# Attention inside a two-layer decoder block: heads scored in blocks of four over four PSUM banks, and the q units confined to one pair of banks

## The reference, cut to what matters

```python
proj = h @ w_in + b_in                       # layer 0
s = q k^T - slope * dist                     # two blocks of 128 queries
m = max(max(s), sink); e = exp(s - m)
p = e / (sum(e) + exp(sink - m))
o = p v;  mix = o @ w_o + b_o
...
proj = h @ w_in                              # layer 1
p_cmp = masked_softmax(q k_cmp^T - slope * d_cmp)
p_sel = masked_softmax(...);  p_win = masked_softmax(...)
o = g0 * p_cmp v_cmp + g1 * p_sel v_sel + g2 * p_win v_win
mix = o @ w_o
...
x = x + rmsnorm(mix);  x = x + rmsnorm(conv_ffn(rmsnorm(x)))
```

## Time and profile before

| | |
|---|---|
| median of 3 runs | 2155.23 us (2155.08 to 2158.4) |
| the profiled execution | 2156.59 us, span of the core 2154.9 us |
| mean granted clock of PE | 0.998 |
| PE busy | 2142.0 us, 99% of the span |
| DVE, ACT, POOL busy | 1330.8, 1067.6, 206.8 us |
| the chain that ended last | PE 97%, DVE 2%, ACT 1% |
| attention stretches (first host slot to the last output) | 57.8 to about 200 us in layer 0, 1138.1 to about 1336 us in layer 1 |

### The profile page before, as it was taken

How to read it: one execution, slowest core, us unless ns; L and a number is a source line. 1 busy time by engine, 2 the same in 40 slices (tenths; PEclk the granted TensorE clock), 3 DMA queues, 4 the chain that set the end, 5 groups by cost and what they waited for, 6 DMA issues and landing times.

```text
span 2154.9 us, 34701 instructions
## 1 busy us (share of the span) xinstructions
PE 2142.0 (99%) x12323; PEld 1833.1 (85%) x12323; DVE 1330.8 (62%) x2019; ACT 1067.6 (50%) x1611; POOL 206.8 (10%) x355
## 2 busy tenths in 40 slices
PE   9999999999999999999999999999999999999999
PEld 9987788888888888888898887788888888888887
DVE  7655676676766754446855554576676666754443
ACT  6675464444444444434556666464444444444343
POOL 3231000000000000002103442000000000000000
PEclk9999999999999999999999999999999999999999
DMA  7444446555565565554673233545556556565553
GB/s 249 140 164 142 164 166 205 185 184 193 168 204 185 185 214 187 189 191 157 215 237 102 86 109 115 178 166 180 200 175 195 185 181 198 177 214 189 191 185 127
DMA packets 107216, 381.42 MB, mean 177 GB/s; under 512 B 14114, under 2 KB 14578, under 8 KB 106482
## 3 DMA queue, kind: packets, MB, share of 16 engines
q1 hardware_dynamic: 104962, 373.69, 51.6%
q10 hardware_dynamic: 2160, 6.46, 0.8%
HBM read 377.97 MB, written 2.14 MB: 176 GB/s over the span
## 4 chain that ended last, share of the span: by engine, by line
PE 97%; DVE 2%; ACT 1%; DMA 0%; issue 0%; SPq 0%; ACTq 0%; DVEq 0%
PE set L599 32%; PE set L663 31%; PE set L603 16%; PE set L775 10%; PE set L843 1%; PE set L824 1%; PE set L867 1%; PE set L706 1%; PE set L826 0%; PE set L870 0%; PE set L860 0%; DVE block_f L1810 0%; DVE wlo L1467 0%; PE set L904 0%; PE set L905 0%; PE set L815 0%
## 5 line engine op out<-in xcount | busy, mean ns | idle before, releaser
L1467 DVE TENSOR_TENSOR wlo<-raw,whi 128x1024 fp32r<-128x1024 f32 x704 | 856.7, 1227 | 585.0 <-ACT whi L1075 583.4
L1075 ACT ACTIVATE whi<-raw 128x1024 fp32r<-128x1024 f32 x704 | 738.4, 1057 | 729.3 <-PE set L603 351.3
L599 PE MATMUL set<-hs,whi 128*128 128x512 f32 x2944 | 976.2, 396 | 2.0 <-DVE hs L1523 2.0
L603 PE MATMUL set<-hs,wlo 128*128 128x256 f32 x2944 | 697.7, 280 | 0.0
L603 PEld LDWEIGHTS set<-hs,wlo 128*128 128x128 f32 x2944 | 547.2, 188 | 63.1
L599 PEld LDWEIGHTS set<-hs,whi 128*128 128x128 f32 x2944 | 504.5, 188 | 71.5 <-DVE hs L1523 3.2
L663 PE MATMUL set<-whi,hid 128*128 128x512 f32 x1408 | 387.2, 395 | 0.0
L663 PEld LDWEIGHTS set<-whi,hid 128*128 128x128 f32 x1408 | 264.9, 188 | 63.2 <-DVE wlo L1467 0.6
L663 PE MATMUL set<-wlo,hid 128*128 128x512 f32 x704 | 222.6, 395 | 0.0
L775 PE MATMUL set<-hs,whi 128*128 128x256 f32 x1280 | 214.6, 289 | 0.0
L775 PEld LDWEIGHTS set<-hs,whi 128*128 128x128 f32 x1280 | 176.7, 189 | 8.3 <-issue 5.5
(11 more groups left out here) (178 smaller groups left out, 1301.9 us busy)
## 6 DMA issues: line engine op xcount, KB each, us to landing
raw<-in_stream SPq DMA_DIRECT2D x704, 512.0 KB, 3.3
gain_rows<-rows ACTq DMA_DIRECT2D x4, 1024.0 KB, 4.8
xT<-in_x SPq DMA_DIRECT2D x8, 256.0 KB, 7.3
out_y<-out_f SPq DMA_DIRECT2D x3, 512.0 KB, 2.6
bo_rows<-rows ACTq DMA_DIRECT2D x1, 1024.0 KB, 8.1
wg_raw<-in_w_gates ACTq DMA_DIRECT2D x1, 768.0 KB, 5.2
out_y<-out_f SPq DMA_DIRECT2D x2, 256.0 KB, 3.2
w2k_sb<-in_w ACTq DMA_DIRECT2D x2, 128.0 KB, 7.4
```

Source lines behind the costliest of these rows:

```text
L599: return mm(sets[set_of(u)][:, t, 0:2 * w], whi[:, slot, cols], r, start=first, stop=final)
L603: return mm(sets[set_of(u)][:, t, w:2 * w], wlo[:, slot, cols], r[:, 0:w], start=False, stop=False)
L1075: A(whi[:, slot, :], raw[:, slot, :], ACT.Copy).then_inc(hi_ready, 1)
L1467: V.tensor_tensor(wlo[:, slot, :], raw[:, slot, :], whi[:, slot, :].bitcast(F32), ALU.subtract).then_inc(lo_ready, 1)
```

## The change

Two pairs of heads make a block (8 blocks in layer 0, 16 in layer 1). PE makes the scores of the block's four heads in one run in four banks, banks 0 and 1 of `set1` and banks 2 and 3 of `set0`, and right behind them the outputs of the block two before. The four turns of the block before stand one by one in later slots. `block_slots` writes down by hand in which slot each block starts (`at`), at which offsets ACT and DVE take its heads (`scored`), and at which offsets the turns stand (`turned`). The compressed scores of layer 1 get a slot of their own, three slots ahead of the block (two in the last group). `turned` moves into the space of `half`, `probs` is twice as large.

Since `set0` banks 2 and 3 now hold scores, all q units accumulate in banks 0 and 1. PE's first products of a q unit wait for the first half of the q read of the unit before, its seventh product waits for the second half (slots 0 and 1). The first output unit waits for the whole of the last q read, in layer 0 with its bias. The second output unit waits for DVE to have read the last scores.

```diff
+def block_slots(layer):
+
+    if layer == 0:
+        at = [CH * UT * g + o for g in range(GROUPS - 1) for o in (4, 18)]
+        scored, turned = [(0, 3, 6, 9)] * len(at), [(1, 4, 7, 10)] * len(at)
+        last = (3, 12)
+        scored, turned = scored + [(0, 2, 4, 6)] * 4, turned + [(1, 3, 5, 7)] * 4
+    else:
+        at = [CH * UT * g + o for g in range(GROUPS - 1) for o in (6, 13, 20, 26)]
+        scored, turned = [(0, 2, 3, 5)] * len(at), [(1, 3, 4, 5)] * len(at)
+        last = (4, 9, 14, 19)
+        scored, turned = scored + [(0, 1, 3, 4)] * 4 + [(0, 2, 3, 5)] * 2, turned + [(1, 2, 3, 4)] * 4 + [(1, 3, 5, 7)] * 2
+    at += [CH * UT * (GROUPS - 1) + o for o in last + (26, 36)]
+    return at, scored, turned
...
+    for b in range(BLOCKS[layer] + 2):
+        first_of_group = layer == 1 and b % 4 == 0 and b < BLOCKS[layer]
+        if first_of_group:
+            put(scoring, at[b] - (3 if b // 4 < GROUPS - 1 else 2), (b, COMPRESSED))
+        if layer == 1 and b % 4 == 1 and b < BLOCKS[layer]:
+            put(turning, at[b], (b - 1, COMPRESSED))
+        for k in range(4):
+            put(scoring, at[b] + scored[b][k], (b, k))
+            if 1 <= b <= BLOCKS[layer]:
+                put(turning, at[b] + turned[b][k], (b - 1, k))
+    return scoring, turning
...
-        ps_scores = [sets[1][:, 0, :], sets[1][:, 1, :]]
+        ps_scores = [[sets[1][:, 0, :], sets[1][:, 1, :]], [sets[0][:, 2, :], sets[0][:, 3, :]]]
...
-                            pe.wait_ge(evacuated, UT * (u - 1))
+                            pe.wait_ge(evacuated, UT * (u if u in (O0, O1) else u - 1))
...
+                    if (k, c) == (1, 0):
+                        pe.wait_ge(scores_read, items_through(0 if u == O0 else 1, PAIRS[0 if u == O0 else 1] - 1))
...
-                    if kt == KT - 1:
+                    if kt == KT - 1 or kt == 0 and u not in (KS1, KW1):
...
-                            if u in (Q0 + 1, KW1):
-                                pe.wait_ge(rnorm_ready, 1 if u < KW1 else 3)
-                            if u in (Q1, Q1 + 1):
-                                pe.wait_ge(evacuated, UT * ((KS1 if u == Q1 else KW1) + 1))
-                            elif u in (Q0 + 2, Q0 + 3, Q1 + 2, Q1 + 3):
-                                pe.wait_ge(evacuated, UT * (u - 1))
+                            if u == KW1:
+                                pe.wait_ge(rnorm_ready, 3)
+                            if u == Q1:
+                                pe.wait_ge(evacuated, UT * (KS1 + 1))
+                        if kt == 0 and n in (0, 6):
+
+                            if Q0 < u < O0:
+                                pe.wait_ge(q_scaled, UT * (u - Q0 - 1) + (2 if n == 0 else 4))
+                            if Q1 < u < O1:
+                                pe.wait_ge(evacuated, UT * (u - 1) + (2 if n == 0 else 4))
...
-                second = u == KW1 or (u - (Q0 if u < O0 else Q1)) % 2 == 1 and u != KS1
-                return [2, 3] if second else [0, 1]
+                return [2, 3] if u == KW1 else [0, 1]
...
-                    for m, h in at[tile]:
-                        if LAG <= m < PAIRS[layer] + LAG and h < len(pair_heads(layer, m - LAG)):
-                            turn(m - LAG, h)
-                        if h == 0 and m < PAIRS[layer]:
-                            scores(m)
-                        if h == 0 and LAG + 1 <= m:
-                            outputs(m - LAG - 1)
+                    for b, k in scoring[tile]:
+                        if k == COMPRESSED:
+                            scores(compressed_pair(b), 0)
+                        if k == 0 and b < BLOCKS[layer]:
+                            for n, m in enumerate(block_pairs(layer, b)):
+                                scores(m, n)
+                        if k == 0 and b >= 2:
+                            if layer == 1 and (b - 2) % 4 == 0:
+                                outputs(compressed_pair(b - 2), 0)
+                            for n, m in enumerate(block_pairs(layer, b - 2)):
+                                outputs(m, n)
+                    for b, k in turning[tile]:
+                        if k == COMPRESSED:
+                            turn(compressed_pair(b), 0)
+                        else:
+                            turn(block_pairs(layer, b)[k // 2], k % 2)
...
-                        o = m - LAG - 1
-                        if h == 1 and o >= 0 and pair_item(layer, o)[1] in ("swa", "win"):
-                            pair_high(o)
-                        if LAG <= m < PAIRS[layer] + LAG and h < len(pair_heads(layer, m - LAG)):
-                            copy_turned(m - LAG, h)
-                        if m < PAIRS[layer] and h < len(pair_heads(layer, m)):
-                            exponents(m, h)
+                    for b, k in turning[tile]:
+                        if k == COMPRESSED:
+                            copy_turned(compressed_pair(b), 0)
+                        else:
+                            copy_turned(block_pairs(layer, b)[k // 2], k % 2)
+                    for b, k in scoring[tile]:
+                        if k == COMPRESSED:
+                            continue
+                        if k == 0 and b < BLOCKS[layer] and layer == 1 and b % 4 == 0:
+                            exponents(compressed_pair(b), 0)
+                        if b < BLOCKS[layer]:
+                            exponents(block_pairs(layer, b)[k // 2], k % 2)
+                        if k == 1 and b >= 2:
+                            pairs = block_pairs(layer, b - 2)
+                            act.wait_ge(o_ready, items_through(layer, pairs[1]))
+                            for n, m in enumerate(pairs):
+                                if pair_item(layer, m)[1] != "sel":
+                                    pair_high(m, n)
...
-                        if h == 0:
-                            if 1 <= m < PAIRS[layer] + 1:
-                                reciprocals(m - 1)
-                            if m < PAIRS[layer]:
-                                for k in range(len(pair_heads(layer, m))):
-                                    add_bias(m, k)
+                    for b, k in scoring[tile]:
+                        if k == COMPRESSED:
+                            add_bias(compressed_pair(b), 0)
                             continue
-                        o = m - LAG - 1
-                        if o >= 0 and pair_item(layer, o)[1] in ("swa", "win"):
-                            pair_low(o)
+                        if k == 0 and 1 <= b <= BLOCKS[layer]:
+                            reciprocals(block_pairs(layer, b - 1)[1])
+                        if k == 1 and layer == 1 and b % 4 == 0 and b < BLOCKS[layer]:
+                            reciprocals(compressed_pair(b))
+                        if b < BLOCKS[layer]:
+                            if k == 2:
+                                reciprocals(block_pairs(layer, b)[0])
+                            add_bias(block_pairs(layer, b)[k // 2], k % 2)
+                        if k == 2 and b >= 2:
+                            for n, m in enumerate(block_pairs(layer, b - 2)):
+                                if pair_item(layer, m)[1] != "sel":
+                                    pair_low(m, n)
...
+                        if g > 0:
+                            dve.wait_ge(scores_ready, items_before(layer, g))
+                        bank = sets[0][:, half_unit, :]
```

More of the change, by code:

```diff
@@ new lines, in attention_steps, with put @@
+def attention_steps(layer):
+    slots = CH * UT
+    at, scored, turned = block_slots(layer)
+    hosts = [[[] for _ in range(slots)] for _ in range(GROUPS - 1)] + [[[] for _ in range(LAST_SLOT + 1)]]
+    scoring = hosts
+    turning = [[[] for _ in h] for h in hosts]
+    def put(where, slot, what):
+        host = min(slot // slots, GROUPS - 1)
+        where[host][slot - host * slots].append(what)
+    for b in range(BLOCKS[layer] + 2):
[9 more added lines that the diff above has]
+    return scoring, turning
@@ L1218, in attention @@
             def attention(layer, host):
-                at = attention_steps(layer)[host]
+                scoring, turning = [steps[host] for steps in attention_steps(layer)]
                 def copy_turned(m, h):
```

117 lines of the change are left out of this document (60 added, 57 removed).

## The result

The changed kernel takes **2181.5 us** (median of 4 runs, 2176.7 to 2182.1) against 2156.7 for the kernel before (4 runs): a ratio of 1.0112, 95% interval 1.0101 to 1.0124. It is slower by 1.1%, 1.5 us under the forecast of 2183. The profiled execution has a span of 2180.4 us, 25.5 more than before.

The account below looks back on a forecast made before the run. PE's own queue was taken as the bound. Saving -5, removed wait -0.7, layer 0 waits +12.6, layer 1 +18.9, correction -0.8 made +25; clock +3 gave +28 on 2156.6, 2184.6, less 1.4 for the median: 2183 us, range 2169 to 2193.

Parts of the forecast that it names:

- The waits at the q units: Layer 0, third and fourth q unit and first output unit: PE waits 2.7, 2.7 and 4.4 us for q read or bias.
- The waits for copies: Layer 1: turns wait for ACT's copies behind exponents and splits; with q read and score waits, 18.9 us in all.
- with 0.8 taken off: Correction of 0.8 us, because walking the kernel before gave waits of 1.1 and 0.5 where its trace has 0.7 and nothing.
- the signs: What would show it: waits about 30 us, about 1 us at layer 1's unit starts, a block's run about 3.5 us.
- The saving on PE: Both layers: fewer entries and exits of attention runs save 5 us in all, ends 2 and 9.
- one run of 2 x 1.65: PE's run per block: scores and outputs of two pairs priced at 1.65 us per pair, before entry and exit.
- The clock: Behind three waits of 2.7 us or more the granted clock falls, 1.7 us lost each: 3 us, ends 0 and 5.1.
- the removed one: Layer 0, first output unit: the 0.7 us wait of the fifth chunk for a stored output goes.
- The rule against the trace: Scores in different row halves and banks could run in parallel by the skill's rule: 20 us back, 2163; 3 in 100.
- The waits were not hidden: Rival that waits are hidden and only the saving stays, making the kernel faster: 2150 us; chance 6 in 100.
- no third of them vanished: Rival that the walk overstates, a third to half of the waits vanishing: +9 to +16, 2164 to 2171; chance 13.
- that rival: Clock falls after waits of 1 to 2 us too: eight more, 1.7 us each, up to 2197; chance 8.

Follow-up runs that it names:

- e1: Changed kernel with DVE's q read moved ahead of the low split of the chunk before last, in all host units of both layers: 2170.9 us.
- e7: Changed kernel with one number changed, the second block of a host unit of layer 0 at slot 16 instead of 18: 2173.5 us.
- e4: Changed kernel with only layer 0's table of slots changed (second block at 17, output unit blocks at 0, 12, 23, 34): 2165.6 us.
- e3: Changed kernel with only layer 1's table of slots changed (a pair's two heads taken together, last blocks respaced): 2168.6 us.
- again: Changed kernel once more, unchanged, for another profiled execution: 2180.5 us.
- e6: Changed kernel with layer 0's new table, layer 1's shifted again, q read and gate inversion moved, first output unit of layer 0 not waiting for q bias: 2153.2 us.
- e8: Kernel with both tables and everything moved, but each run takes scores, outputs, scores, outputs pair by pair: 2159.7 us.
- e12: Kernel before, with the score products of both heads of a pair on the first head's rows: 2186.3 us.
- e2: Kernel before with only the q units' banks changed to a single set, with the changed kernel's waits for read and q bias: 2163.8 us.
- e5: Changed kernel with both new tables of slots, layer 0's and layer 1's: 2156.4 us.
- e9: Kernel with both tables and everything moved, with score products of both heads of a pair on the first head's rows: 2182.0 us.

## Why the prediction was right, and where it was not

**The waits at the q units** were walked at 2.7, 2.7 and 4.4. They are marked 2.56, 2.53 and 4.39; read as above, they are 2.72, 2.69 and 4.55. Chain, place and size were right, shown by moving the read (e1), the block (e7) and the table (e4). All waits of layer 0 were put at 12.6 and are 11.8.

**The waits for copies** were right in place and cause, shown by e3. Layer 1 was walked at 18.9, with 0.8 taken off, and lost 16.7 in marked waits. By host unit: 5.9 forecast, 5.1 marked in five waits, so 5.9; then 4.2 forecast each, 2.83 and 2.87 marked in four waits each, so 3.5; then 4.5 against 2.98 marked in five, 3.8. The walked waits for the reads of the third and fourth unit are not marked, but PE's timeline has them:

```profile
1199.91 0.28 PE L830 MATMUL set<-hs,wlo 128*128 128x256 f32 x1
1200.33 0.50 PE L830 MATMUL set<-hs,whi 128*128 128x256 f32 x2
```

The start comes 0.41 after the product before it instead of 0.12: 0.29 lost here and 0.30 at 1250.22, 0.6 of the missing 1.4 us. They are not the "about 1 us" that the signs gave for these places. Where the other 0.8 went stays open.

**The saving on PE** was put at 5, ends 2 and 9. For the same code of layer 0 the stretch less its waits is 201.6, 199.7 and 198.3 us with 14.1, 10.1 and 6.8 us of work at 1.2 GHz (changed kernel, again, e3), 0.45 us for each of these. Drawn on to none this is about 195.2, an estimate from three profiles, against 198.6 before; e1, with 3.4 us at 1.2 GHz and two unmarked waits of 0.3, gives 195.3. In layer 1, e1 had full clock and 251.6 against 256.8. That is 8.6 saved, with unmarked waits still in it, and 9.1 in e6. The step that failed is "one run of 2 x 1.65": the row is 2.96, and a block's run with its entry (0.09, as taken) and its exit is 3.2 and not the "about 3.5" of the signs. The change of shape inside the run, which I let in only at the upper end ("at most 0.08 each"), costs 0.17 each time (e8) and carries 6.8 us. The fewer entries and exits, which I had counted as the whole saving, carry 2.3, 1.8 in layer 0 and 0.5 in layer 1, so both terms of the sum were mis-sized, and 8.6 lies inside the ends only because the upper one was wide. Why layer 1 gains so little from them, no run shows.

**The clock** was put at 3, ends 0 and 5.1, for three waits. By the same sums it cost 6.4 in layer 0 and 1.5 in layer 1, 7.9 us: above my upper end. Three things were off. I had priced a fall at 1.7 us, as if half the work of 3.4 us were lost; it was 1.5 in four profiles that fell behind the wait of 2.1 in layer 1 (253.1 to 253.2 against 251.6 in e1). I had counted three such waits, and this was a fourth. And I had taken each fall to last as long as the one I had seen. The wait ahead of the stretch in the earlier trace rows, 2.66 to 2.68 us, stands in all fourteen profiles; the clock fell at it or right behind it each time, for 3.4 us in nine of them and for 6.8 in five. In the second profile of the changed kernel each of the four falls in the two attention stretches lasted 3.4 us, and by the same sums the clock cost 6.0.

So +25.5 of span is 27.7 more of waits (30.0 forecast, the removed one and the 0.8 counted), 7.9 of clock (3), 8.6 saved (5), and 1 to 1.5 gained in stretches that the change does not touch. The error of 5 in the clock ran against those of 2 in the waits and 4 in the saving. That the total is within 2 us is luck; that the kernel got slower, and by the waits, is not.

**The rule against the trace** was weighed wrongly. I read from scores and outputs that "take their full 1.65 us" that nothing runs side by side, but had no row for what the serial time would be. It is 1.50 for one pair's scores alone (e12). The Trainium skill, page TensorEngine Tiling (Array Packing), section Key Properties, says that different tiles execute in parallel; these runs agree, at 0.85 us (97.67 to 98.52, where the outputs start) for what takes 1.50 in one half of the rows, and 1.46 for outputs that take 2.74 in one half of the columns. What I priced as a rival of -20 us was already in the kernel before, so my answer to it, "the pairs did not overlap before", was false, and the sum stood for another reason: no gain was left to have. The trace of the kernel before shows it without any run. Cut off at 97.70, right behind the start of the scores, its timeline has two products that together last 0.49 us; that of e12, where both heads use the same rows, cut off at 101.20, has only one, and it alone lasts 0.48:

```profile
97.67 0.49 PE L824 MATMUL set<-k_dup,qg 64*128 64x256 f32 x2
101.18 0.48 PE L824 MATMUL set<-k_dup,qg 64*128 64x256 f32 x1
```

The row of four in the earlier trace rows merges them, and hides that they start together. The same section of the Trainium skill says that a change of tiling mode drains the engine; the 0.35 us for two changes in e8 is a price that fits it.

**The rivals.** The waits were not hidden, and no third of them vanished: 28.5 us of the 31.5 walked are there. The clock fell more than forecast, but not behind the waits of 1 to 2 us, as that rival had it.

## What to carry to other kernels

A read that frees a bank belongs in front of everything on its engine that waits for another engine: here one low split ahead of it cost 7 us of waits and, with the clock behind them, some 10 us of time. When one engine waits for short pieces of another's queue, move what stands ahead of the piece before blaming the amount of work: tables of slots alone took the waits from 24.7 to 5.5 us. And before saying that products do not overlap, look at when each single one starts, or make them unable to (same rows, same columns) and time that.

## What the runs showed of the hardware

- Two products of 64 rows in different halves of the array's rows, or with 64 columns in different halves of its columns, run almost entirely side by side: 0.85 against 1.50 us for a pair's scores, 28.8 to 30.0 us over 48 pairs.
- Going between score products (64 rows, 128 columns) and output products (128 rows, 64 columns) costs PE about 0.17 us each time.
- Behind a wait of PE of 2.1 to 4.4 us the granted clock fell in 14 of 17 cases over seven profiles, not in three (2.12 in e1, 2.56 in e2, 2.52 in e3), and twice behind a wait of 0.89 (e5, e9), where the ten other profiles with this wait kept full clock in that place. Behind two waits of 0.72 and 0.68 at the end of layer 0 it fell in three profiles (before, e9, e12). The same kernel spent 20.5 us at 1.2 GHz in one execution and 13.7 in another, with the same waits. By the sums above a microsecond of work at the low level cost 0.45 us; the low level can also run down while PE still waits, 2.9 us in the first profile, and that part costs nothing.
